# A decoder layer's opening stage: five uneven column chunks, eight tile buffers, and sums placed between projection units

## The reference

```python
mod = (silu(c) @ w_ada + b_ada)                   # w_ada is (2048, 6 * 2048)
sh1, sc1, g1, sh2, sc2, g2 = jnp.split(mod, 6, axis=-1)
h = x * (1.0 + sc1) + sh1                         # x is (512, 2048)
proj = h @ w_in                                   # w_in is (2048, ...); then attention and scan
...
```

## Time and profile before

| | |
|---|---|
| median of 3 runs | 3396.45 us (3391.7 to 3397.94) |
| the profiled execution, its own time | 3397.14 us |
| its span in the trace | 3395.4 us |
| PE busy over the span | 3160.7 us (93%) |
| DVE, ACT, POOL busy | 2383.3, 1058.0, 999.2 us |
| first product of unit 32 | at 192.78 us of the span |

### The profile page before, as it was taken

The page is one execution under the profiler, slowest core; times in us unless marked ns, Lnnn a source line. Parts: engine busy times, 40 slices in busy tenths (PEclk is TensorE's granted clock), DMA queues, the critical chain, the costliest instruction groups (busy, mean ns, idle before and its releaser), DMA issues.

```text
span 3395.4 us, 44427 instructions
## 1 busy us (share of the span) xinstructions
PE 3160.7 (93%) x16301; PEld 2676.5 (79%) x16301; DVE 2383.3 (70%) x3389; ACT 1058.0 (31%) x1591; POOL 999.2 (29%) x734
## 2 busy tenths in 40 slices
PE   5899999999699999995999999999999999999993
PEld 2576788666548999995777789998999999899982
DVE  1242464753707999984788777878787787878888
ACT  1132355421304343331222233323333333333332
POOL 0010000000005635532222223334343443435550
PEclk9899999999899999997999999999999999999997
DMA  8766213456034455555888878888888888888983
GB/s 313 268 235 246 82 60 129 146 200 246 11 114 147 144 187 172 167 201 185 288 262 283 286 263 292 286 305 297 291 304 296 309 281 304 296 293 314 339 322 161
DMA packets 272632, 791.82 MB, mean 233 GB/s; under 512 B 118128, under 2 KB 130544, under 8 KB 226544
## 3 DMA queue, kind: packets, MB, share of 16 engines
q1 hardware_dynamic: 215024, 462.66, 42.1%
q0 software_dynamic: 50560, 317.87, 25.0%
q10 hardware_dynamic: 6912, 9.44, 0.8%
HBM read 746.91 MB, written 42.99 MB: 233 GB/s over the span
## 4 chain that ended last, share of the span: by engine, by line
PE 79%; DVE 14%; DMA 4%; issue 1%; ACT 1%; SPq 1%; POOL 0%; ACTq 0%; DVEq 0%; POOLq 0%
PE ps L2099 29%; PE ps L2026 26%; PE ps L1765 13%; PE ps L2001 3%; DVE arena L1544 3%; DMA arena<-in_w_ada 2%; PE ps L1730 2%; PE ps L1789 1%; DVE arena L1541 1%; DVE arena L1570 1%; PE ps L2047 1%; PE ps L1824 1%; DVE arena L1296 1%; PE ps L1703 1%; DVE arena L1454 1%
## 5 line engine op out<-in xcount | busy, mean ns | idle before, releaser
L2099 PE MATMUL ps<-split,w_parts 128*128 128x512 f32 x4608 | 1063.3, 391 | 67.3 <-DVE split L1620 38.2
L2099 PEld LDWEIGHTS ps<-split,w_parts 128*128 128x128 f32 x4608 | 864.0, 188 | 255.6 <-DVE split L1620 39.8
L2026 PE MATMUL ps<-h_parts,split 128*128 128x384 f32 x5376 | 947.4, 335 | 1.4 <-POOL split L744 1.4
L2026 PEld LDWEIGHTS ps<-h_parts,split 128*128 128x128 f32 x5376 | 933.8, 188 | 5.1 <-issue 1.6
L1058 ACT ACTIVATE split<-below_parts 128x1024 fp32r<-128x1024 f32 x416 | 441.6, 1062 | 1220.7 <-PE ps L2099 701.5
L1620 DVE TENSOR_TENSOR split<-below_parts,split 128x1024 fp32r<-128x1024 f32 x416 | 509.1, 1224 | 316.1 <-ACT split L1058 311.3
L756 POOL COPY arena<-arena 128x1 uint32 x256 | 182.8, 714 | 885.7 <-DVE arena L1594 494.5
L1152 DVE TENSOR_TENSOR win_parts<-arena,win_parts 128x512 fp32r<-128x512 f32 (+2 forms) x208 | 129.4, 630 | 307.9 <-ACT win_parts L807 299.4
L1575 DVE CUSTOM_DVE_ANT_0 arena<-arena 128x2048 f32<-128x2048 f32 x128 | 292.4, 2285 | 33.4 <-DMA arena<-in_u_tab,arena 33.4
L1594 DVE SCALAR_TENSOR_TENSOR arena<-arena 128x2048 f32<-128x2048 f32 x128 | 300.4, 2347 | 3.4 <-DVE arena L1586 2.4
L759 POOL DMA_INDIRECT arena<-in_v_tab,arena x128 | 251.3, 1963 | 106.8 <-POOL arena L756 101.9
(11 more groups left out here) (256 smaller groups left out, 3221.0 us busy)
## 6 DMA issues: line engine op xcount, KB each, us to landing
below_parts<-in_u_units SPq DMA_DIRECT2D x256, 512.0 KB, 4.6
below_parts<-in_v_tab SPq DMA_DIRECT2D x256, 512.0 KB, 6.8
arena<-in_w_ada SPq DMA_DIRECT2D x96, 1024.0 KB, 6.8
arena<-in_w_slices POOLq DMA_DIRECT2D x56, 512.0 KB, 3.9
gates_by_expert<-arena SPq DMA_DIRECT2D x24, 1024.0 KB, 4.8
below_parts<-gates_by_expert SPq DMA_DIRECT2D x32, 768.0 KB, 9.0
arena<-in_w_out POOLq DMA_DIRECT2D x32, 512.0 KB, 4.6
acts_ahead<-arena ACTq DMA_DIRECT2D x48, 192.0 KB, 2.1
```

The source lines that it names most:

```text
L2026: ins = nc.tensor.matmul(ps[:, 6 + b, 0:DT], lhs[:, cols], h2_parts[:, rhs, k, :], start=k == 0 and n == 0, stop=k == KT - 1 and n == 2)
L2099: ins = nc.tensor.matmul(ps[:, 2 * m + b, :], w_parts[:, buf, lhs, i, m * P:(m + 1) * P], rhs[:, b * 512:(b + 1) * 512], start=i == 0 and ...
```

## The change

The chunks become five, of 2, 2, 4, 4 and 4 row tiles (`WIDTHS`; `KS[c]` are the row tiles of chunk c). A chunk of w row tiles has w + w tiles of `w_ada`. All tiles keep their size of 1 MB; for w = 2 a tile has 1024 rows by 256 columns, in pieces of 1 KB. The number of tiles in all stays 32. The tiles go through eight buffers: the four of `ada`, and four more in memory that is written later. `x` is loaded in two pieces: row tiles 0 to 3 after the first two tiles, the others after part (1, 0)'s tiles. PE, ACT and DVE take the parts, the copies of rows and the sums after given units, by two tables. The number of units, their products and their slices stay as they were, only their order follows the new chunks. Later loads of `w_ada` still go through the four buffers of `ada`.

```diff
-CHUNKS = 4
-CW = D // CHUNKS
-CK = KT // CHUNKS
+WIDTHS = (2, 2, 4, 4, 4)
+CHUNKS = len(WIDTHS)
+GROUPED = 4
+CW = D // GROUPED
+ADAS = 8
...
-FIRST_UNITS = [(s, k) for c in range(CHUNKS) for s in range(2) for k in range(c * CK, (c + 1) * CK)]
+KS = [range(sum(WIDTHS[:c]), sum(WIDTHS[:c + 1])) for c in range(CHUNKS)]
+FIRST_UNITS = [(s, k) for c in range(CHUNKS) for s in range(2) for k in KS[c]]
+PARTS_AFTER = {0: ((1, 0),), 1: ((1, 1),), 6: ((2, 0),), 7: ((2, 1),), 9: ((3, 0),), 11: ((3, 1),), 17: ((4, 0),), 19: ((4, 1),)}
+X_PARTS = ((0, KS[2][0]), (KS[2][0], KT))
+SUMS_AFTER = {1: 1, 7: 2, 12: 3, 20: 4}
...
+        chunk_ada = [ada[:, i, :] for i in range(4)] + [at(o, D) for o in (XCX, XCX + D, KVDT, KVDT + D)]
+        first_tile = [sum(WIDTHS[:c]) * 2 for c in range(CHUNKS)]
...
-                n = (c * 2 + m) * CHUNKS + j
-                if n >= 4:
-                    sp.wait_ge(ada_used, n - 3)
...
+                w = WIDTHS[c]
+                n = first_tile[c] + m * w + j
+                if n >= ADAS:
+                    sp.wait_ge(ada_used, n - ADAS + 1)
+                rows, cols = D // w, m * D + KS[c][0] * P
...
-                    if c == 0 and m == 0:
-                        sp.dma_start(h_cols[:, :, :], x_cols[:, :, :]).then_inc(x_loaded, 16)
+                    if m == 0 and c < 2:
+                        first, end = X_PARTS[c]
+                        sp.dma_start(h_cols[:, first:end, :], x_cols[:, first:end, :]).then_inc(x_loaded[c], 16)
...
+            row_copied(0, 0)
+            row_copied(0, 1)
+            chunk_high(0)
+            for n in range(LEFT):
+                high(n + 2)
+                if n in LAST:
+                    evict(n)
+                for c, m in PARTS_AFTER.get(n, ()):
+                    row_copied(c, m)
+                if n in SUMS_AFTER:
+                    chunk_high(SUMS_AFTER[n])
...
+            for n in range(LEFT):
+                low(n + 2)
+                if n in SUMS_AFTER:
+                    chunk_h(SUMS_AFTER[n])
+                    chunk_low(SUMS_AFTER[n])
...
-                    for a in range(CK):
-                        k = j * CK + a
-                        ins = nc.tensor.matmul(ps[32 * a:32 * a + 32, 7, :], c_act[:, k:k + 1].to_broadcast([P, 32]), ada[:, n % 4, a * CW:(a + 1) * CW],
-                                               start=j == 0, stop=j == CHUNKS - 1, tile_position=(0, 32 * a))
+                    for a in range(KT // w):
+                        k, at_group = j * (KT // w) + a, a % GROUPED
+                        ins = nc.tensor.matmul(ps[32 * at_group:32 * at_group + 32, 7, 0:w * P], c_act[:, k:k + 1].to_broadcast([P, 32]),
+                                               chunk_ada[n % ADAS][:, a * w * P:(a + 1) * w * P],
+                                               start=k < GROUPED, stop=k >= KT - GROUPED, tile_position=(0, 32 * at_group))
...
             for n in range(LEFT):
-                after = n // (2 * CK) + 1
-                if n % (2 * CK) == CK and after < CHUNKS:
-                    chunk_part(after, 0)
                 unit_at(n)
-                if n % (2 * CK) == 2 * CK - 1 and after < CHUNKS:
-                    chunk_part(after, 1)
-                    chunk_mod_sums(after)
+                for c, m in PARTS_AFTER.get(n, ()):
+                    chunk_part(c, m)
+                if n in SUMS_AFTER:
+                    chunk_mod_sums(SUMS_AFTER[n])
```

More of the change, by code:

```diff
@@ L507, in decoder_layer @@
         c_loaded = sem("c_loaded")
-        x_loaded = sem("x_loaded")
-        ada_full = [sem(f"ada_full{i}") for i in range(4)]
+        x_loaded = [sem(f"x_loaded{i}") for i in range(2)]
+        ada_full = [sem(f"ada_full{i}") for i in range(ADAS)]
         ada_used = sem("ada_used")
@@ L591, in later_load @@
                     sp.wait_ge(ada_used, tile - 3)
-                    to, full = ada[:, tile % 4, :], ada_full[tile % 4]
+                    to, full = ada[:, n % 4, :], ada_full[n % 4]
                 else:
@@ L1129, in chunk_h @@
                 dve.wait_ge(mod_ready, c + 1)
[L1130 to L1132 removed]
+                dve.wait_ge(x_loaded[min(c // 2, 1)], 16)
+                for k in KS[c]:
                     nc.vector.tensor_scalar(h_cols[:, k, :], h_cols[:, k, :], mod_cols[:, KT + k:KT + k + 1], mod_cols[:, k:k + 1],
@@ L1136, in chunk_low @@
             def chunk_low(c):
-                for k in range(c * CK, (c + 1) * CK):
+                for k in KS[c]:
                     dve.wait_ge(h_high, k + 1)
@@ L1417, in beside @@
                     own(nc.vector.tensor_scalar(ln1bb, ln1bb, ALPHA, None, ALU.mult))
[L1419 to L1426, removed]
+            chunk_h(0)
+            chunk_low(0)
+            low(0)
+            low(1)
+            for n in range(LEFT):
[3 more added lines that the diff above has]
+                    chunk_low(SUMS_AFTER[n])
+            dve.wait_ge(ada_used, 2 * KT)
             dve.wait_ge(consts, 18)
@@ L1692, in chunk_part @@
             def chunk_part(c, m):
-                for j in range(CHUNKS):
-                    n = (c * 2 + m) * CHUNKS + j
-                    pe.wait_ge(ada_full[n % 4], 16 * (n // 4 + 1))
+                w = WIDTHS[c]
+                for j in range(w):
+                    n = first_tile[c] + m * w + j
+                    pe.wait_ge(ada_full[n % ADAS], 16 * (n // ADAS + 1))
                     if j == 0 and c and m == 0:
@@ L1710, in chunk_mod_sums @@
                 for m in range(2):
[L1711 to L1714, removed]
+                    for i, k in enumerate(KS[c]):
+                        ins = nc.tensor.matmul(ps[:, 7, m * KT + k:m * KT + k + 1], chunk_acc[:, c % 2, m, i * P:(i + 1) * P], firsts[:, :], start=True, stop=True)
                 ins.then_inc(mod_sum, 1)
@@ L1720, in later_part @@
                 if n < 2 * KT:
-                    what, full, count = ada[:, tile % 4, :], ada_full[tile % 4], 16 * (tile // 4 + 1)
+                    what, full, count = ada[:, n % 4, :], ada_full[n % 4], 16 * (2 * KT // ADAS + n // 4 + 1)
                 else:
-                    what, full, count = later_ada[:, tile % 2, :], ada_full[tile % 2], 16 * (KT + (n - 2 * KT) // 2 + 1)
+                    what, full, count = later_ada[:, tile % 2, :], ada_full[tile % 2], 16 * (2 * KT // ADAS + 2 * KT // 4 + (n - 2 * KT) // 2 + 1)
                 if k == 0:
@@ L1728, in later_part @@
                 pe.wait_ge(full, count)
-                for a in range(CHUNKS):
+                for a in range(GROUPED):
                     ins = nc.tensor.matmul(ps[32 * a:32 * a + 32, 7, :], c_act[:, k:k + 1].to_broadcast([P, 32]), what[:, a * CW:(a + 1) * CW],
```

30 lines of the change are left out of this document (12 added, 18 removed).

## The result

The changed kernel takes 3363.74 us in the median of four runs (3360.45 to 3367.74), beside 3395.32 us of the kernel before. The ratio is 0.9904 (95% interval 0.9890 to 0.9918): 1% faster, 32 us. Run again in another series it was 0.9896 (0.9879 to 0.9912).

The account below looks back on a forecast made before the run. PE and the transfers were taken to bound the opening by turns. Chunk by chunk, unit 32 starts at 166.0 instead of 192.78, 26.8 us earlier: 3396.45 - 26.8 = 3369.7 us, range 3361 to 3380.

Parts of the forecast that it names:

- Chunks 0 and 1: Opening's first steps: unit 0 starts at 33.0, not 52.42; PE waits 6.6 us; chunk 1's sums end at 53.1.
- Chunk 2: Opening's next step: units 2 to 7 and chunk 2's tiles, copy, sums and uncovered step; unit 8 starts at 82.8.
- slow start: Units after a PE wait: four take longer than 10.92 us at full clock; 2.1 us extra assumed.
- Chunks 3 and 4: Opening's last step: sums 3.59 us each plus 1.0 each for a lower clock; unit 32 starts at 166.0.
- cover: Queued units hiding moved copies and low parts; without it about 1 us lost at each of two places.
- Dear pieces: Rival on narrow chunks' tile loads: 1 KB pieces make a tile 5.4 us; saved 8, 3389 us; chance 0.09.
- Late slices: Rival on slice loads: they queue behind eight tiles; saved 13 to 23, 3373 to 3383 us; chance 0.05.
- Clock: Rival on PE from unit 1: clock stays at 1.2 GHz, 61 us slower than before, 3457; chance 0.03.
- Lost later: Rival behind unit 32: a later stage loses the saving, time within 0.2% of before; chance 0.02.

Follow-up runs that it names:

- e7: The changed kernel with three quarters of x loaded behind all four tiles of chunk 1 instead of between them; unit 32 at 162.78 us.
- e4: The changed kernel with parts and sums at the places of the kernel before; unit 32 at 171.76 us, ratio 0.9934 to the kernel before.
- e1: The kernel before with eight tile buffers as the only change; unit 32 at 176.51 us, ratio 0.9940 to the kernel before.
- e10: The kernel before with only parts and sums moved between units, four buffers, even chunks; unit 32 at 182.97 us, ratio 0.9965 to the kernel before.
- e8: The changed kernel with the narrow chunks' eight tiles from a host-laid copy in 8 KB pieces; unit 32 at 157.79, median 3366.20 us, ratio 0.9900.
- e6: The changed kernel with the sums of chunks 3 and 4 made twice; run once, unit 32 at 166.28 us.

## Why the prediction came out as it did

The range and the direction were right, and so was the mechanism in the main: transfers and products now run at once, and steps stand between units. The forecast of 3369.7 us was 6 us too high, for a reason that can be named.

**A reading that was wrong, though the sum does not use it.** The prediction says that PE waits 13.9 to 14.5 us for tiles four times, and has nothing left to do while tiles are loaded. These rows are the last tile's time from issue to landing. Behind the first unit of the kernel before, PE idled 9.6 us for tiles in six waits, none over 3.1 us, 8.7 for low parts and 2.1 for copies; that is the 20.4 us named above. The earlier trace rows could have told it, with PE busy in 17.48 of 24.00 us from 68 to 92. What the change takes away is as much the lower clock behind each gap as the gap. The sum of the prediction follows the landing of tiles and PE's work one by one, so it came out all the same.

**Chunks 0 and 1: right.** Unit 0 started at 32.97 (33.0 forecast), the last tile of chunk 1 was read from 49.11 (48.6), the sums of chunk 1 ended at 53.4 (53.1). The wait of 6.6 us came as two, 1.35 and 3.21, with a tile read between them. The price of 1 KB pieces, worked out from pieces of 2 KB and longer as 3.03 us a tile, was 2.88 and 3.02. The Trainium skill's count of cycles (DMA: Bandwidth & Descriptors, section Why small descriptors are slow) had led to an estimate of 2.82; the direction agrees, and the measured price is a little above it.

**Chunk 2: right in sum, by luck.** Unit 8 started at 83.00 (82.8), because errors cancel. Units 2 to 6 took 14.55 us and not 13.7, with a longer slow start (13.61 in the second execution), and part (2, 0) began at 67.97 and not at 66.8 (unit 0 ended 0.9 later too, which the wait behind it hid). The prediction has PE done with chunk 2's tiles at 75.6, but by its own prices it is 72.5 + 3.62 = 76.1. It was 77.4, and PE did not wait for the last tile, since it came later itself (73.80). The sums gave it back, 2.03 us in place of 3.59.

**Chunks 3 and 4: the term that was mis-sized.** I priced the sums at 3.59 us each and the start behind them at 1.0, from rows of before in which sums always stand behind a wait for tiles. They took 1.68 each and no slow start followed: 2 x 1.91 + 2 x 1.0 = 5.8 us, which is the difference between 166.0 and 160.81 but for 0.6 us: unit 8 started 0.2 later, and units and parts took 0.4 more. The runs show why: 3.59 us is the price at half clock. The price follows the granted clock that the profile gives for the sums themselves: 3.59 at 0.50 (before, e7), 2.90 at 0.64 (e4, chunk 2), 2.03 at 0.93 (the changed kernel, chunk 2), 1.96 at 1.00 behind a copy (e1, e4) and 1.68 at 1.00 behind a unit. The price of a row holds for the clock of its place.

**What each part is worth.** The prediction ascribed 19.4 us to the early first unit and spoke of the rest as cover. That split is not what the runs show. The buffers are worth 16.3 us alone and the places 9.8; together they save 33.9, more than the sum, since a part that is moved forward needs its tiles there (places alone left 14.0 us of waits for them, e10). The widths save 3.4 alone, add 4.8 to the buffers, and take 1.9 away from buffers with places, and 0.9 from places alone. Their early start is real. It is lost again because a chunk of two row tiles holds only four units of work, while the next chunk's tiles take longer than that to land: hence the waits that end at 49.11, and no unit left to stand between the sums of chunk 2 and unit 8. e7 and e8 bear this out in part: with the waits ahead of 49.11 gone or shortened, PE waited for chunk 2's tiles instead.

**The rivals.** *Dear pieces*: refuted, 0.2 to 0.3 us a tile over 2 KB; long pieces give 3.0 us by unit 32. *Late slices*: they took 6.6 us to landing in the median and the tiles 13.9, as the DMA issues of the changed kernel show:

```profile
arena<-in_w_ada SPq DMA_DIRECT2D x38, 1024.0 KB, 13.9
arena<-in_w_slices POOLq DMA_DIRECT2D x16, 512.0 KB, 6.6
```

Later than the 4.6 of the earlier trace rows, far from what would hold PE up; no wait of PE for slices is in the chain. By the Trainium skill (DMA: Bandwidth & Descriptors, section Queues, rings and completion order) an engine takes turns between its queues, and these two rows agree with it. *Clock*: the granted clock was 1.00 from 100 us on; the second wait and the open chain show 0.72 (48 to 66) and 0.74 (74 to 86). The mechanism exists: in e7, behind PE's waits for tiles, the sums ran at 0.50. This is what the Trainium skill describes (TensorE: Matmul & The Clock Gate, section HAM oscillation), and the trace agrees. The fall in e6 is another case, with no wait in it. Here the mechanism worked for the change: fewer waits, and small products at their full speed. One piece of evidence against this rival was read wrongly. The earlier trace rows give 1.00 from 52 to 68, but the first products of that stretch start 0.43 us apart (52.99, 53.41, 53.84), as those behind 92.39 do at 0.50, and products at full clock start 0.23 apart (100.17, 100.40). So the column's 1.00 cannot be trusted over the first microseconds of that window, nor for the sums at 45.88, which took 3.59 us. *Lost later*: no, 3202.3 against 3202.6 us.

## What to carry to other kernels

When an engine and the transfers take turns, let both run first (buffers, and the queue's order), and only then shorten the time to the first unit: an early start is worth what follows it without a wait. A chain of small steps across engines is hidden by work that does not need it, placed between the chain's end and its user. When a price is taken from a row, look at the clock and at what stood ahead of that row, for a change that takes a wait away changes the prices behind it too. And a row of a chain that names a transfer is no idle time of the engine: look at the engine's own waits before you call it one.

## What the runs showed of the hardware that I had not expected

Sixteen records of 128 by 1 products took 3.59 us behind a wait of PE for transfers (granted clock 0.50), 1.96 behind a copy (1.00), and 1.68 without any gap (1.00). Behind twice as many (3.46 us) in the midst of dense work the granted clock was 0.62 from 108 to 112 us (one execution, e6), and behind 1.68 us of them it stayed at 1.00. And with eight buffers asked for ahead, the slices on the other queue landed in 6.6 us against 4.6, and the tiles in 13.9 against 9.2: both took about half as long again, and the slices still came well ahead.
